# A two-block transformer kernel: the second block's second layer MLP down by seven products too, its first 512 features by eight

## What is computed

```python
# first block, 2 layers, 512 tokens, width 1024
h = rmsnorm(x, g_mix); z = h @ w_in
x = x + (sigmoid(ga) * (attention(z) @ w_a) + sigmoid(gb) * (retention(z) @ w_b)) @ w_out
x = x + square(relu(rmsnorm(x, g_mlp) @ w_up)) @ w_down
# second block, 2 layers; xc are 256 context tokens beside the 512 of x
for l in range(2):
    need_ctx = l < 1                                # the context is updated in layer 0 only
    h = rmsnorm(x, norm1_g[l]) * (1 + sc1) + sh1    # hc likewise from xc
    y, yc = token_mixers(h @ w_in[l], hc @ w_in[l], ...)
    x = x + g1 * (y @ w_out[l])
    h = rmsnorm(x, norm2_g[l]) * (1 + sc2) + sh2
    x = x + g2 * (square(relu(h @ w_mlp1[l])) @ w_mlp2[l])      # 1024 -> 4096 -> 1024
    # and the same for xc where need_ctx
```

## Time and profile before

| | |
|---|---|
| median of 3 runs | 3332.32 us (3330.84 to 3332.92) |
| profiled execution | 3333.19 us, span 3331.4 us |
| mean granted PE clock | 0.992 |
| busy share of the span | PE 98%, POOL 56%, DVE 54%, ACT 38% |
| queue q1 (SP's) | 257.13 MB, 24.4% of 16 engines |

### The profile page before, as it was taken

One profiled execution on the slowest core, in us unless ns is written; L12 is line 12 of the kernel. 1 busy time (PEld: TensorE's weight loads), 2 busy tenths in 40 slices (PEclk: granted clock), 3 DMA queues, 4 the chain that ended last, 5 costly groups with the idle time before them and its releaser, 6 DMA issues.

```text
span 3331.4 us, 50466 instructions
## 1 busy us (share of the span) xinstructions
PE 3276.1 (98%) x17362; PEld 2739.9 (82%) x17362; DVE 1808.1 (54%) x2893; ACT 1279.7 (38%) x2071; POOL 1857.9 (56%) x2076
## 2 busy tenths in 40 slices
PE   7999999999999999999999999899999999999999
PEld 6778888888778888888888878899998888788887
DVE  4642257788644238778856445576652664442113
ACT  4433242223434233323444553343333445543223
POOL 4435568887434558888465223555554563246555
PEclk9999999999999999999999999999999999999999
DMA  4213345554322335555353112122222442133333
GB/s 172 92 51 98 98 140 189 164 176 134 114 67 76 95 96 188 176 180 175 106 139 92 47 58 89 57 63 70 69 64 68 128 125 67 64 110 107 100 94 108
DMA packets 106429, 358.56 MB, mean 108 GB/s; under 512 B 12000, under 2 KB 22496, under 8 KB 104352
## 3 DMA queue, kind: packets, MB, share of 16 engines
q1 hardware_dynamic: 71712, 257.13, 24.4%
q10 hardware_dynamic: 34560, 99.30, 9.1%
HBM read 336.79 MB, written 8.59 MB: 104 GB/s over the span
## 4 chain that ended last, share of the span: by engine, by line
PE 75%; issue 13%; POOL 9%; DVE 3%; ACT 1%; DMA 0%; POOLq 0%; ACTq 0%; DVEq 0%; SPq 0%
POOL w_lo L652 8%; PE ps L1122 7%; PE ps L1123 6%; PE ps L1124 6%; PE ps L775 5%; PE ps L776 5%; PE ps L777 5%; PE ps L1340 4%; PE ps L1341 4%; PE ps L1342 4%; PE ps L1031 3%; PE ps L1032 3%; PE ps L1033 3%; PE ps L1178 2%; PE ps L1180 2%
## 5 line engine op out<-in xcount | busy, mean ns | idle before, releaser
L652 POOL TENSOR_TENSOR w_lo<-w_raw,w_hi 128x256 fp32r<-128x256 f32 x1904 | 1696.5, 923 | 1333.5 <-ACT w_hi L1713 1319.2
L1713 ACT ACTIVATE w_hi<-w_raw 128x1024 fp32r<-128x1024 f32 x448 | 473.5, 1057 | 674.3 <-DMA w_raw<-in_w 183.6
L775 PE MATMUL ps<-h_hi,w_hi 128*128 128x512 f32 x944 | 374.0, 396 | 0.0
L777 PE MATMUL ps<-h_hi,w_lo 128*128 128x512 f32 x944 | 369.4, 391 | 0.0
L776 PE MATMUL ps<-h_lo,w_hi 128*128 128x512 f32 x944 | 369.3, 391 | 0.0
L2652 DVE SCALAR_TENSOR_TENSOR ada_junk<-ada_w,c_silu 128x1024 f32<-128x1024 f32 x192 | 315.9, 1645 | 3.3
L1340 PE MATMUL ps<-c_hi,w_hi 128*128 128x512 f32 (+1 forms) x832 | 298.9, 359 | 3.5 <-DVE vm L2911 1.8
L1341 PE MATMUL ps<-c_lo,w_hi 128*128 128x512 f32 (+1 forms) x832 | 286.8, 345 | 0.0
L1342 PE MATMUL ps<-c_hi,w_lo 128*128 128x512 f32 (+1 forms) x832 | 286.7, 345 | 0.0
L1122 PE MATMUL ps<-c_hi,w_hi 128*128 128x512 f32 (+1 forms) x792 | 279.4, 353 | 2.8 <-DVE c_lo L2823 2.8
L1123 PE MATMUL ps<-c_lo,w_hi 128*128 128x512 f32 (+1 forms) x792 | 278.6, 352 | 0.0
(11 more groups left out here) (421 smaller groups left out, 6614.4 us busy)
## 6 DMA issues: line engine op xcount, KB each, us to landing
w_raw<-in_w SPq DMA_DIRECT2D x476, 512.0 KB, 3.5
ada_w<-in_ada ACTq DMA_DIRECT2D x96, 512.0 KB, 3.7
zs<-stage ACTq DMA_DIRECT2D x52, 128.0 KB, 2.1
m_row<-m_spill ACTq DMA_DIRECT2D x16, 384.0 KB, 5.4
wq_row<-wq_spill ACTq DMA_DIRECT2D x16, 384.0 KB, 5.4
x_spill<-x ACTq DMA_DIRECT2D x2, 2048.0 KB, 7.2
zs_m<-zm ACTq DMA_DIRECT2D x32, 128.0 KB, 2.1
bias<-in_rpb ACTq DMA_DIRECT2D x8, 512.0 KB, 3.7
```

What stands on the lines that cost most here:

```text
L652: last = nc.gpsimd.tensor_tensor(w_lo[:, j, c], w_raw[:, j % RAW, c], w_hi[:, j, c].bitcast(F), ALU.subtract)
L775: nc.tensor.matmul(bank, w_hi[:, j, w], rhs_hi[:, k, :], start=(k == 0), stop=False)
L777: last = nc.tensor.matmul(bank, w_lo[:, j, w], rhs_hi[:, k, :], start=False, stop=(k == n - 1))
L1713: nc.scalar.activation(w_hi[:, j, :], w_raw[:, j % RAW, :], ACT.Copy).then_inc(hi_ready, 1)
```

## The change

SEVENS becomes (0, 1), so layer 1's MLP also goes by sevens, with `wide` 256. In both layers the first of the six blocks is now done by eight plain block products (`down_in_eights`: 48 matmuls of `wide` columns a chunk), with tokens split but no sums of tokens or of weights; five blocks by sevens follow. Chunk order and weights stay as they are in layer 0; in layer 1 the stream is laid out likewise. Counters get offsets for this.

At the start chunk 0 is loaded ahead of x, x comes in four pieces, chunk 1 after it. ACT loads its table and splits chunk 0 first, makes all eight h_hi, then the squares with chunk 1's split after the first. PE does three matmuls on zeros, then chunk 0 in an order that uses the lo part of the weights three tiles late; chunk 1 comes before the row sums, chunk 2 before the spread. The tables' semaphores become one. PE's loop over the first block's layers is written out. `values_by_token` stands before DVE's first unit.

```diff
-SEVENS = (0,)
+SEVENS = (0, 1)
...
             sp.dma_start(vec[:, :], dram["vec"]).then_inc(vec_loaded, 16)
-            for j in range(2):
-                half_x = slice(j * HALF_KT, (j + 1) * HALF_KT)
-                sp.dma_start(x[:, half_x, :], dram["x"][:, half_x, :]).then_inc(x_loaded[j], 16)
-                sp.dma_start(w_raw[:, j, :], dram["w"][j, :, :]).then_inc(raw_ready[j], 16)
+            sp.dma_start(w_raw[:, 0, :], dram["w"][0, :, :]).then_inc(raw_ready[0], 16)
+            for j in range(KT // 2):
+                two = slice(2 * j, 2 * j + 2)
+                sp.dma_start(x[:, two, :], dram["x"][:, two, :]).then_inc(x_loaded[j], 16)
+            sp.dma_start(w_raw[:, 1, :], dram["w"][1, :, :]).then_inc(raw_ready[1], 16)
...
+            def very_first_chunk():
...
+                pe.wait_ge(eps_set, 2)
+                for i in range(WARM):
+                    nc.tensor.matmul(ps[:, 7, :], tmp_3[:, 0, 0:P], tmp_3[:, 0, :], start=True, stop=True)
+                pe.wait_ge(hi_ready, 1)
+                pe.wait_ge(bank_read[0], 2)
+                for k in range(KT):
+                    pe.wait_ge(hhi_ready, k + 1)
+                    term(w_hi, h_hi, k, start=(k == 0))
+                    pe.wait_ge(hlo_ready, k + 1)
+                    term(w_hi, h_lo, k)
+                    if k >= 3:
+                        pe.wait_ge(lo_ready, 1)
+                        term(w_lo, h_hi, k - 3)
...
+                if l == 0:
+                    very_first_chunk()
+                    chunk(g0, 1, h_hi, h_lo)
+                else:
+                    first_chunk(g0, 0, 2 * l)
                 pe.wait_ge(c0_loaded, 16)
                 sums_mix(l)
...
+            def down_in_eights(L, g, need_ctx):
...
+                normed(g + 1, 0, need_ctx)
+                for m in range(BLOCK_FF):
+                    at, j = down_at(g, m)
+                    arrive(at, j)
+                    if m == 0:
+                        pe.wait_ge(bank_read[2], g + 3)
+                        pe.wait_ge(tokens_lo, tokens_before(L) + 4)
...
+                    for out in range(2):
+                        for h in range(2):
+                            bank = ps[:, PLAIN_BANKS[m % 2][2 * out + h], 0:wide]
+                            for i in range(4):
+                                e, half = i // 2, i % 2
...
+                                nc.tensor.matmul(bank, w_hi[:, j, w], t_h, start=(i == 0), stop=False)
+                                nc.tensor.matmul(bank, w_hi[:, j, w], t_l, start=False, stop=False)
+                                last = nc.tensor.matmul(bank, w_lo[:, j, w], t_h, start=False, stop=(i == 3))
...
             def mlp_by_sevens(L, g, need_ctx):
 
-                down_by_sevens(L, 0, g, need_ctx)
+                down_in_eights(L, g, need_ctx)
+                up_after_eights(g + 2, need_ctx)
                 with pe.Fori(1, HALF_BLOCKS) as b:
-                    up_after_sevens(L, b, g + b * 2, need_ctx)
                     down_by_sevens(L, b, g + b * 2, need_ctx)
-                up_after_sevens(L, HALF_BLOCKS, g + 2 * HALF_BLOCKS, need_ctx)
+                    up_after_sevens(L, b, g + b * 2 + 2, need_ctx)
...
+            act.wait_ge(eps_set, 1)
+            nc.scalar.activation(tiny[:, 0, 0:1], eps[:, 0:1], ACT.Square)
+            first_split(0)
             act.wait_ge(layer_vec, 1)
-            for j in range(2):
-                act.wait_ge(x_loaded[j], 16)
-                prepare(j * HALF_KT, gain_mix)
-                first_split(j)
-                for k in range(1, HALF_KT):
-                    prepare(j * HALF_KT + k, gain_mix)
+            for k in range(KT):
+                act.wait_ge(x_loaded[k // 2], 16)
+                nc.scalar.activation(h_hi[:, k, :], x[:, k, :], ACT.Identity, scale=gain_mix[:, k:k + 1]).then_inc(hhi_ready, 1)
+            for k in range(KT):
+                nc.scalar.activation(squares[k], x[:, k, :], ACT.Square).then_inc(sq_ready, 1)
+                if k == 0:
+                    first_split(1)
...
                 def mlp_by_sevens(L, g):
 
-                    positive(g, 0)
-                    split(g, 0)
-                    block_of_sevens(L, 0, g)
+                    wide = wide_half(need_ctx)
+                    for i in range(BLOCK_FF):
+                        if i >= 2:
+                            act.wait_ge(tokens_lo, tokens_before(L) + i - 1)
+                        positive(g, i)
+                        split(g, i)
+                        act.wait_ge(v2_ready, squares_before(L) + i + 1)
+                        nc.scalar.activation(t_hi[:, i // 2, i % 2 * 2:i % 2 * 2 + 2, 0:wide],
+                                             hid[:, i % 2 * 2 * wide:(i % 2 + 1) * 2 * wide].rearrange("p (q t) -> p q t", q=2), ACT.Copy).then_inc(tokens_hi, 1)
...
+                values_by_token()
                 for u in range(N_ATT):
...
-                    if u == 1:
-                        values_by_token()
...
+                def block_in_eights(g):
...
+                    for m in range(BLOCK_FF):
+                        at, j = down_at(g, m)
+                        for i in range(4):
...
+                            onto = onto_second if i % 2 else onto_first
+                            onto(2 * m + i // 2, PLAIN_BANKS[m % 2][i]).then_inc(seventh_read if i < 3 else bank_read[j], 1)
```

More of the change, by code:

```diff
@@ L369, in sem @@
             return ctx.enter_context(nc.semaphore(name))
-        x_loaded = [sem(f"x_loaded{j}") for j in range(2)]
-        vec_loaded, c0_loaded, c1_loaded = sem("vec_loaded"), sem("c0_loaded"), sem("c1_loaded")
+        x_loaded = [sem(f"x_loaded{j}") for j in range(KT // 2)]
+        vec_loaded, c0_loaded, tables_loaded = sem("vec_loaded"), sem("c0_loaded"), sem("tables_loaded")
         raw_ready = [sem(f"raw_ready{j}") for j in range(RAW)]
@@ L466, in hybrid_then_dit @@
         ADDS = KT - HALF_KT - 1 + KT - 2
+        WARM = 3
         ROT_TILES, RET_TILES = (3, 2), (RET_HEADS, RET_HEADS)
@@ L735, in lower_sevens @@
                     lower(g, j)
-                lower(g + 1, 0)
-                with pool.Fori(0, HALF_BLOCKS) as b:
+                for m in range(-1, 2 * BLOCK_FF):
+                    lower(g + 1 + (m + 1) // RING, (m + 1) % RING)
+                with pool.Fori(1, HALF_BLOCKS) as b:
                     for m in range(BLOCK_FF):
@@ L841, in transposed, with term @@
                 last.then_inc(vt_ready, 1)
-            with pe.Fori(0, DEPTH) as l:
-                g0 = l * G1
-                first_chunk(g0, 0, 2 * l)
+            def very_first_chunk():
+                def term(w, h, k, start=False, stop=False):
+                    return nc.tensor.matmul(ps[:, 0, :], w[:, 0, k * P:(k + 1) * P], h[:, k, :], start=start, stop=stop)
+                pe.wait_ge(eps_set, 2)
[11 more added lines that the diff above has]
+                        term(w_lo, h_hi, k - 3)
+                for k in range(KT - 3, KT):
+                    last = term(w_lo, h_hi, k, stop=(k == KT - 1))
+                last.then_inc(chunk_used, 1)
+            for l in range(DEPTH):
+                g0 = l * G1
+                if l == 0:
[3 more added lines that the diff above has]
+                    first_chunk(g0, 0, 2 * l)
                 pe.wait_ge(c0_loaded, 16)
                 sums_mix(l)
-                chunk(g0, 1, h_hi, h_lo)
-                spread(2 * l)
-                chunk(g0, 2, h_hi, h_lo)
+                if l:
+                    chunk(g0, 1, h_hi, h_lo)
+                    spread(2 * l)
+                    chunk(g0, 2, h_hi, h_lo)
+                else:
+                    chunk(g0, 2, h_hi, h_lo)
+                    spread(2 * l)
                 chunk(g0, 3, h_hi, h_lo)
@@ L893, in finish @@
                     last.then_inc(rturn_ready, 1)
-                pe.wait_ge(c1_loaded, 16)
+                pe.wait_ge(tables_loaded, 16)
                 pe.wait_ge(rb_copied, 2 * l + 1)
@@ L1679, in _ @@
                 g0 = START_2 + L * G2
-                pe.wait_ge(c2_loaded, 16)
+                pe.wait_ge(tables_loaded, 32)
                 attention(L, need_ctx, first, g0)
@@ L3208, in _ @@
             dve.wait_ge(mod_ready, 2)
-            dve.wait_ge(c2_loaded, 16)
+            dve.wait_ge(tables_loaded, 32)
             for L in range(DEPTH):
```

98 lines of the change are left out of this document (65 added, 33 removed).

## The result

The changed kernel takes 3348.51 us (median of 5 runs, 3346.06 to 3350.23), the one before 3332.92 (3330.84 to 3335.63). The ratio is 1.0046, 95% interval [1.0032, 1.0061]: slower, by 15.6 us. The forecast was 3348. The profiled execution took 3348.51 too, with a span of 3346.7.

A forecast was written before the change was run, and what follows sets the result against it. It took TensorE, busy 98%, as the bound, with the ACT, POOL and DVE chain level beside it in blocks by sevens. 3333.2 - 4.5 - 4 - 9.4 + 0.9 + 4 + 25 + 3 = 3348.2, stated as 3348; range 3317 to 3367.

The forecast's parts named there:

- Start: Start of the kernel: products begin near 7.2 us and chunk 3 at 35.5 to 37.5; -4.5 us (-7 to 0).
- Products on zeros: Start of the kernel: three warm products before 3 us, with idle behind, are given nothing.
- Values by token: Attention, each layer: moving DVE's av before unit 0 returns 2.0 of TensorE's 2.25 us wait; -4 us (-4.5 to 0).
- The wait named as late next: Attention, each layer: once av is early, p_ready is late next, 0.7 us earlier than now.
- First layer, block 0 by eights: First layer's MLP, block 0: 33.6 us without part sums instead of 42.96; -9.4 us (-9.7 to -4).
- ramp: Second layer's MLP, before the first down chunk: TensorE waits for all four tiles of tokens; +4 us (0 to +7).
- eights: Second layer's MLP, first 512 features: four chunks by eights at 5.67 us instead of 5.44; +0.9 us.
- clock: Second layer's MLP: TensorE's clock falls after new waits; +3 us for the stage (0 to +24).
- Five blocks: Second layer's five blocks by sevens: 48.5 us each, TensorE waiting on ACT, POOL and DVE; +25 us.
- hidden chain: Rival, second layer's blocks: DVE sums in POOL's gaps, so the ninth product is in time; 3309 us, chance 0.14.
- One stretch of lower clock per block: Rival, second layer's blocks: a low-clock stretch costs 4.8 us in each; 3369 us, chance 0.13.
- The chain that shrinks with the tokens: Rival, second layer's blocks: token steps fall to two thirds, chain 25.8 us, block 45.7; 3333 us, chance 0.18.

The follow-up runs named there:

- repeated-product run: Changed kernel with the first block product of each second-layer block by sevens made four times instead of once; 3347.36 us, ratio 1.0040.
- both cuts: Changed kernel, second layer's blocks 2 to 5: POOL's subtractions 16 of 256 elements wide, DVE adding 128 of 256 columns of each product to x; 3321.83 us.

## Why the prediction was right

It held in the total (3348 against 3348.51) and in its mechanism. Its terms one by one, with what the traces show:

- **Start, -4.5.** -6.5 in the profiled execution. Nine more traces with the same start have their first scores at 55.38 to 57.70 us instead of 61.76, eight of them from 56.77, so -4.1 to -5.0. The usual value is the predicted one; the profiled execution was lucky, and in its clock: from 20 to 40 us it was granted 0.91, as was the trace with 55.38, and the other eight 0.83. The first product starts at 8.04 (predicted 7.2), chunk 1 waits for w_lo until 16.70 (16.6), chunk 3 starts at 34.31 (35.5 to 37.5).
- **Products on zeros, 0.** Not settled, 1.7 us by one trace, as told. I had put them before 3 us; they take from 1.50 to 6.90.
- **Values by token, -4.** -3.9 by the landmarks (10.4 less 6.5), 4.5 when undone. The wait named as late next is there: 0.48 and 0.41 us for p_sb. Between ctx_sum and the second block's down products another 1.0 is gained that I didn't predict. Behind ctx_sum the granted clock was higher, 0.87 from 1580 to 1620 us against 0.83 from 1590 to 1630 in the kernel before; whether that is the whole of it is open.
- **First layer, block 0 by eights, -9.4.** -9.7: 33.29 us where I had 33.6. Blocks 1 to 5 stayed: 63.06 us for the one shown, 62.98 in the earlier trace rows.
- **Second layer, ramp +4, eights +0.9, clock +3.** TensorE waits 3.27 us for DVE's t_lo at 2980.53, where I had 4. Its 192 products of 256 columns take 25.74 us, at 0.118 they would take 22.7: 3 us went to the lower clock, granted 0.88 in that window. With 0.7 in two of the blocks that is 4.4 for my 3, and most of it fell here and not in the blocks.
- **Five blocks, +25.** +29.5. The step that was mis-sized is the pace behind the ninth product: I let products come every 0.709, "which DVE's 0.42 and about 0.3 of hand-over just follow". A read takes 0.48, the way there 0.20 and back 0.06, 0.74 in all, and with the lost overlap of the weight load the mean is 0.78. That is 15.45 instead of 14.2 us in the block from 3055.40 and 6 us over the five. The chain was slightly shorter than predicted, 28.0 to 28.1 us for 28.6, which takes 3 back. The wait for w_lo was 0.23 us instead of 1.2. TensorE's idle time is 3.7 us and not 6.9, mostly because part of the chain's time passed at the lower clock.

The sum of the stage is 36.0 against my 33, and the profiled start's extra 2 us covers most of the difference. So the total agrees better than the terms do, by luck.

The rivals: the hidden chain (3309) would have needed sums of 0.41 us for the third chunk; they are 0.94. One stretch of lower clock per block (3369) was there in all five, but mostly in a place where TensorE would else have waited for DVE; in the repeated-product run the granted clock was 1.00 through a block and the block no shorter (49.19). The chain that shrinks with the tokens (3333) wanted 25.8 us and blocks of 45.7; they are 28.1 and 49.4. Its ground fails on the part sums cut to an eighth, 0.77 us.

What I hadn't asked is what the blocks would take with the chain gone. I took 41.6, which is 0.5 short even with both cuts (42.15), since a product takes 0.72 us and not 0.709. Even with POOL's subtractions nearly out, they take 43.7, more than the 43.52 before: at 256 columns a product by sevens is so short that the hand-over (1.5 us) eats most of the 1.9 that the seventh was to save.

## What to carry to other kernels

Trading TensorE products for sums on DVE asks for long products: at 384 columns the chain (32.6 us of its own) and TensorE (33.4) were level; at 256 the chain fell only to 28.1 and TensorE's part to 21.7. Before a wait between two engines is removed, ask whether they exclude each other at the memory: the wait may be the time in which the other one runs undisturbed, and a second buffer then gives back little, here 1.07 of 2.52 us. Then see where TensorE's clock falls: a stretch at the lower clock costs nothing while TensorE would wait anyway, and its full price once the wait is gone. And where a bank is handed over and back, compare the whole round (start of the read, read, return) with the product's length, since a shortfall of 0.02 us (0.74 for the round, 0.72 for the product) shows nowhere as idle time and still costs 8% of the pace.

## What the runs showed that I had not expected

- The second sum buffer removed a wait of 2.52 us per block and the time didn't move (ratio 1.0049 against 1.0046), though the one block at clock 1.00 was 1.1 us shorter.
- Sums of 32 columns and of 256 start about every 0.71 and 0.88 us under POOL's subtractions, 0.11 and 0.34 without. POOL's own instruction is 0.92 beside the wide sums and 0.74 beside the narrow ones. So both pay, POOL by about 0.2.
- Memsets of 240 elements by POOL take about 0.25 us each and leave DVE's sums at 0.41 to 0.43.
- DVE's reads of the products, one input in PSUM and one in SBUF, take 0.48 us beside POOL's subtractions too (3150.61 above) and 0.48 with POOL idle. The sums and t_lo, which were held up, have both inputs in SBUF.
- The same start code put the first scores anywhere from 55.27 to 57.70 us in ten traces. The two below 56 were granted a clock of 0.91 from 20 to 40 us, the other eight 0.83. A gain of 2 us at the start can't be read from one trace.
- TensorE's granted clock was 0.50 for a few us in each of the changed kernel's five blocks, after waits of 2.49 and 0.46 to 0.95 us; while it lasted, products came every 1.28 us instead of 0.72. In the block from 3055.40 it ended by the ninth product and cost nothing; in that from 3104.54 it lasted into the tenth and cost 0.7 us.
